# Column quarters of TensorE for the recurrence's diagonal and lower levels, and fp32 attention values by column halves

## What is computed

```python
def _chunked_gated_recurrence(q, k, v, log_f, s0):
    '''S_t = diag(f_t) S_{t-1} + k_t v_t^T ; o_t = S_t^T q_t (per head), chunkwise exact.'''
...
        b = jnp.cumsum(lc, axis=2)
        o = jnp.einsum('bhtd,bhde->bhte', qc * jnp.exp(b), S)
...
        a = jnp.einsum('bhtd,bhsd,bhtsd->bhts', qc, kc, decay)
        o = o + jnp.einsum('bhts,bhse->bhte', a, vc)
...
def _sink_attention(q, k, v, mask, sinks):
    s = jnp.einsum('bnqkgd,bnskd->bnkgqs', q, k) * scale
...
    m = jnp.maximum(jnp.max(s, axis=-1, keepdims=True), sink)
    p = jnp.where(valid, jnp.exp(s - m), 0.0)
    denom = jnp.sum(p, axis=-1, keepdims=True) + jnp.exp(sink - m)
    return jnp.einsum('bnkgqs,bnskd->bnqkgd', p / denom, v)
```

## Time and profile before

| | us |
|---|---|
| median of 3 runs | 1123.98 (1123.93 to 1124.26) |
| profiled execution | 1123.76 |
| its span | 1121.9 |
| PE busy in it | 1085.6 (97%) |
| DVE, POOL, ACT busy | 615.8, 436.7, 399.2 |

### The profile page before, as it was taken

One profiled execution on the slowest core, in us unless ns is written; L12 is line 12 of the kernel. 1 busy time (PEld: TensorE's weight loads), 2 busy tenths in 40 slices (PEclk: granted clock), 3 DMA queues, 4 the chain that ended last, 5 costly groups with the idle time before them and its releaser, 6 DMA issues.

```text
span 1121.9 us, 18648 instructions
## 1 busy us (share of the span) xinstructions
PE 1085.6 (97%) x7464; PEld 1046.8 (93%) x7464; DVE 615.8 (55%) x1222; ACT 399.2 (36%) x807; POOL 436.7 (39%) x294
## 2 busy tenths in 40 slices
PE   6999999999999999999999999999989999999996
PEld 4899999999999999999999999999989999888896
DVE  7143636363635353544673225447677777987835
ACT  4412121212121212354433222431017767755522
POOL 1245454545353535361114452243544433332233
PEclk9999999999999999999999999999999989999999
DMA  7111111111111111101123342321112113232103
GB/s 269 39 38 39 59 39 60 38 60 38 60 39 59 39 60 38 60 20 60 50 88 114 131 135 75 125 69 57 39 39 80 60 58 89 77 80 66 46 26 126
DMA packets 39797, 76.85 MB, mean 69 GB/s; under 512 B 5792, under 2 KB 24736, under 8 KB 39584
## 3 DMA queue, kind: packets, MB, share of 16 engines
q1 hardware_dynamic: 39712, 75.67, 20.7%
HBM read 58.12 MB, written 17.54 MB: 67 GB/s over the span
## 4 chain that ended last, share of the span: by engine, by line
PE 77%; DVE 11%; ACT 7%; issue 2%; POOL 1%; DMA 0%; DVEq 0%; SPq 0%; ACTq 0%; POOLq 0%
PE G L1569 51%; PE R L1619 6%; PE G L1815 4%; ACT SP L982 4%; DVE SP L1407 3%; PE R L1607 2%; DVE PTL L1423 2%; DVE QNL L1392 2%; PE R L1668 1%; PE R L1661 1%; PE R L1635 1%; PE R L1646 1%; PE R L1596 1%; PE R L1628 1%; PE R L1654 1%
## 5 line engine op out<-in xcount | busy, mean ns | idle before, releaser
L1569 PE MATMUL G<-XH,WH 128*128 128x344 f32 x1176 | 385.5, 328 | 1.9 <-DVE RAWF L1078 1.9
L1569 PE MATMUL G<-XL,WH 128*128 128x344 f32 x1176 | 377.9, 321 | 2.3 <-DVE KE L1377 1.9
L1569 PE MATMUL G<-XH,WL 128*128 128x344 f32 x744 | 237.7, 319 | 0.0
L1569 PEld LDWEIGHTS G<-XL,WH 128*128 128x128 f32 x1176 | 221.7, 189 | 5.0 <-DVE WL L1068 2.2
L1569 PEld LDWEIGHTS G<-XH,WH 128*128 128x128 f32 x1176 | 221.9, 189 | 4.3 <-issue 2.1
L612 POOL TENSOR_TENSOR WL<-WR,WH 128x1024 fp32r<-128x1024 f32 x40 | 102.2, 2556 | 181.7 <-ACT WH L757 181.7
L757 ACT ACTIVATE WH<-WR 128x1024 fp32r<-128x1024 f32 x58 | 61.1, 1055 | 289.7 <-PE G L1569 195.2
L1569 PEld LDWEIGHTS G<-XH,WL 128*128 128x128 f32 x744 | 139.8, 188 | 0.0
L1569 PE MATMUL G<-XL,WL 128*128 128x344 f32 x432 | 139.1, 322 | 0.0
L643 POOL TENSOR_TENSOR K<-K,FP 128x512 f32<-128x512 f32 x48 | 78.1, 1628 | 122.2 <-PE R L1619 122.2
L695 POOL TENSOR_TENSOR SP<-SP,small 128x1024 f32<-128x1024 f32 (+1 forms) x32 | 57.3, 1791 | 134.7 <-DVE small L1418 134.7
(11 more groups left out here) (259 smaller groups left out, 2161.0 us busy)
## 6 DMA issues: line engine op xcount, KB each, us to landing
WR<-w SPq DMA_DIRECT2D x58, 512.0 KB, 3.7
A<-x SPq DMA_DIRECT2D x8, 516.0 KB, 8.7
RESO<-x SPq DMA_DIRECT2D x8, 516.0 KB, 5.0
h_spill<-H SPq DMA_DIRECT2D x8, 516.0 KB, 2.9
gate_spill<-EV SPq DMA_DIRECT2D x24, 172.0 KB, 1.9
RES<-h_spill SPq DMA_DIRECT2D x24, 172.0 KB, 2.6
y<-H SPq DMA_DIRECT2D x24, 172.0 KB, 1.9
SS<-states SPq DMA_DIRECT2D x8, 512.0 KB, 3.5
```

Of the source, the lines that this page charges most:

```text
L1569: return nc.tensor.matmul(G[unit_bank(NU * n + i)][:, 0:TU], w[:, n % 3, k, :], x[:, seg(i)], start=(k == 0 and p == 0), stop=(k == KT - 1 ...
```

## The change

The diagonal and levels 1 to 4 (h = 2 to 16) compute, per chunk, only the four blocks of 32 keys against the queries of the same 32 tokens: each a matmul of its own with at most 32 weight columns, whose output lies on the PSUM partitions of that quarter (0, 32, 64, 96). Level 5 (h = 32) goes by two halves of 64 tokens with 32 weight columns each. Level 6 is unchanged. `QM` is laid out by quarters (32 queries, 16 odd ones). DVE's merges read the new layout with as many elements as before. All five R banks are cleared by DVE at the start, since the merges read rows that no matmul has written.

In the attention the values are taken as fp32 from one copy: V in `VP`, the probabilities in `PT`. Each key block has two matmuls, one per half of heads, with 64 weight columns and output on PSUM partitions 0 to 63 or 64 to 127. ACT copies the turned block before (`copy_before`), DVE the own (`copy_own`), each waiting for its transposes and for the values that last read `PT`. The zero fields, the low parts and their subtractions are gone.

```diff
     G3 = sb("G3", [P, T], fp32, [ra[0]])
-    QM = sb("QM", [P, NC, 192], fp32, ra)
+    QM = sb("QM", [P, 4 * NC, 48], fp32, ra)
     r1 = [ra[0]]
...
     rb_[0] += 2 * 4 * SEQ
-    VPH, VPL = sb("VPH", [P, NC, 192], fp32r, rb_), sb("VPL", [P, NC, 192], fp32r, rb_)
+    VP = sb("VP", [P, NC, P], fp32, [rb_[0]])
+    rb_[0] += 2 * 4 * NC * 192
     WXH, WXL = sb("WXH", [P, 2, HK, P], fp32r, [rb_[0]]), sb("WXL", [P, 2, HK, P], fp32r, [rb_[0] + 4 * T])
     EV, EV2 = sb("EV", [P, T], fp32, rb_), sb("EV2", [P, T], fp32, rb_)
     rk = [rb_[0]]
     RES = [sb(f"RES{i}", [P, T], fp32, rb_) for i in range(2)]
     rc = [rb_[0]]
     SP_ = [sb(f"SP{i}", [P, 4, 256], fp32, rb_) for i in range(2)]
-    PTH, PTL = sb("PTH", [P, 2, 512], fp32r, rb_), sb("PTL", [P, 2, 512], fp32r, rb_)
+    PT = sb("PT", [P, 2, 512], fp32, rb_)
     QNH, QNL = sb("QNH", [P, 2, 2, P], fp32r, rb_), sb("QNL", [P, 2, 2, P], fp32r, rb_)
...
         return t[:, 2 * p:2 * p + 2, nb * P:(nb + 1) * P]
+
+    def before_count(q):
+
+        return q - q // NC

...

-        def turned_high(q):
-            for kb in key_blocks(q):
-                act.wait_ge(pt_done, pt_count(q, kb))
-                if q:
-                    act.wait_ge(pv_done, q)
-                nc.scalar.activation(PTH[:, kb, :], R[2 + kb][:], ACT.Copy).then_inc(pth_done, 1)
+        def copy_before(q):
+
+            if q % NC:
+                act.wait_ge(pt_done, pt_count(q, 0))
+                act.wait_ge(pv_done, q)
+                nc.scalar.activation(PT[:, 0, :], R[2][:], ACT.Copy).then_inc(pt_before, 1)

...

-            b = bank(r, f"D{i}")[:, 0:2 * 192].rearrange("p (c w) -> p c w", c=2)
-            at = AT[:, 2 * i:2 * i + 2]
+            b = bank(r, f"D{i}")[:, 0:2 * 192].rearrange("p (c v w) -> p c v w", c=2, v=4)
+            at = AT[:, 2 * i:2 * i + 2].rearrange("p c (v w) -> p c v w", v=4)
             dve.wait_ge(group_done, group_value(r, f"D{i}"))
             if READ_COUNT[f"D{i}", r] > 2:
                 dve.wait_ge(read_dve, READ_COUNT[f"D{i}", r] - 2)
-            nc.vector.copy_predicated(at, imask[:].unsqueeze(1).broadcast_to([P, 2, P]), b[:, :, 0:P]).then_inc(read_dve, 1)
+            nc.vector.copy_predicated(at, imask[:].rearrange("p (v w) -> p v w", v=4).unsqueeze(1).broadcast_to([P, 2, 4, 32]),
+                                      b[:, :, :, 0:32]).then_inc(read_dve, 1)
             dve.wait_ge(read_dve, READ_COUNT[f"D{i}", r] - 1)
-            nc.vector.copy_predicated(at[:, :, 1:P:2], lmask[:, 0, :].unsqueeze(1).broadcast_to([P, 2, P // 2]),
-                                      b[:, :, P:192]).then_inc(read_dve, 1)
+            nc.vector.copy_predicated(at[:, :, :, 1:32:2],
+                                      lmask[:, 0, :].rearrange("p (v w) -> p v w", v=4).unsqueeze(1).broadcast_to([P, 2, 4, 16]),
+                                      b[:, :, :, 32:48]).then_inc(read_dve, 1)

...

+        for b in R:
+            nc.vector.memset(b[:], 0.0)
         nc.vector.memset(ones[:], 1.0)
...
                 if j == 0 and i == 0:
-                    for c in range(2):
-                        dve.wait_ge(vp_high, c + 1)
-                        view = [t[:, 4 * c:4 * c + 4].rearrange("p c (z w) -> p c z w", z=3)[:, :, 0:3:2, :]
-                                for t in (VPH, VPL)]
-                        nc.vector.tensor_tensor(view[1], R[3 + c][:].rearrange("p (c v w) -> p c v w", c=4, v=2),
-                                                view[0].bitcast(fp32), ALU.subtract).then_inc(vp_done, 1)
                     dve.wait_ge(v_turned, 3)
...

-        def turned_rest(q):
-            for kb in key_blocks(q):
-                dve.wait_ge(pth_done, pt_count(q, kb))
-                nc.vector.tensor_tensor(PTL[:, kb, :], R[2 + kb][:], PTH[:, kb, :].bitcast(fp32), ALU.subtract
-                                        ).then_inc(pt_read, 1)
+        def copy_own(q):
+
+            dve.wait_ge(pt_done, pt_count(q, 1))
+            if q:
+                dve.wait_ge(pv_done, q)
+            nc.vector.tensor_copy(PT[:, 1, :], R[3][:]).then_inc(pt_own, 1)

...
                     at = 2 * i + c
-                    ins = nc.tensor.matmul(b[:, c * 192:(c + 1) * 192], K[r % 2][:, at * P:(at + 1) * P], QM[:, at, :],
-                                           start=True, stop=True)
+                    for v in range(4):
+                        ins = nc.tensor.matmul(b[32 * v:32 * v + 32, 192 * c + 48 * v:192 * c + 48 * v + 48],
+                                               K[r % 2][:, at * P + 32 * v:at * P + 32 * v + 32], QM[:, 4 * at + v, :],
+                                               start=True, stop=True)
                 ins.then_inc(group_done, 1)
...
             b = open_group(r, f"L{l}")
+            w = max(32, 2 * h)
             for c in range(NC):
-                cols = slice(c * P, (c + 1) * P)
-                keys = slice(c * P, (c + 1) * P - h)
-                ins = nc.tensor.matmul(b[0:P - h, c * 64:(c + 1) * 64].rearrange("p (n h) -> p n h", h=h),
-                                       K[r % 2][:, keys],
-                                       by_blocks(QU[:, cols], l)[:, :, 1, :], start=True, stop=True)
+                for v in range(P // w):
+                    first = c * P + v * w
+                    ins = nc.tensor.matmul(b[v * w:v * w + w - h, first // 2:(first + w) // 2].rearrange(
+                                               "p (n h) -> p n h", h=h),
+                                           K[r % 2][:, first:first + w - h],
+                                           by_blocks(QU[:, first:first + w], l)[:, :, 1, :], start=True, stop=True)
             ins.then_inc(group_done, 1)
...
             for kb in key_blocks(q):
-                if q:
-                    pe.wait_ge(pt_read, pt_count(q - 1, 1))
+                if kb and q:
+                    pe.wait_ge(pt_own, q)
+                if not kb and q > 1:
+                    pe.wait_ge(pt_before, before_count(q - 1))
                 for i in range(4):
...
             p, nb = query(q)
-            pe.wait_ge(pt_read, pt_count(q, 1))
+            pe.wait_ge(pt_own, q + 1)
+            if nb:
+                pe.wait_ge(pt_before, before_count(q))
             if q:
                 pe.wait_ge(gated, q)
-            steps = [(v, kb, a, b) for kb in key_blocks(q) for v in range(2)
-                     for a, b in ((VPH, PTH), (VPH, PTL), (VPL, PTH))]
-            for n, (v, kb, a, b) in enumerate(steps):
-                ins = nc.tensor.matmul(R[4][:, 0:2 * P].rearrange("p (j w) -> p j w", j=2),
-                                       a[:, nb - 1 + kb, 64 * v:64 * v + P],
-                                       b[:, kb, :].rearrange("p (j v w) -> p j v w", j=2, v=2)[:, :, v, :],
-                                       start=(n == 0), stop=(n == len(steps) - 1))
+            blocks = key_blocks(q)
+            for kb in blocks:
+                for v in range(2):
+                    rows = slice(64 * v, 64 * v + 64)
+                    ins = nc.tensor.matmul(R[4][rows, 0:2 * P].rearrange("p (j w) -> p j w", j=2),
+                                           VP[:, nb - 1 + kb, rows],
+                                           PT[:, kb, :].rearrange("p (j v w) -> p j v w", j=2, v=2)[:, :, v, :],
+                                           start=(kb == blocks[0]), stop=(kb == 1))
             ins.then_inc(pv_done, 1)
```

More of the change, by code:

```diff
@@ L1111, in first_query @@
                 dve.wait_ge(group_done, group_value(r - 1, "O1"))
[L1112 to L1116 removed]
+            odd = QM[:, :, 32:48]
+            gates = FG[:, 0:SEQ].rearrange("p (c n two) -> p c n two", n=16, two=2)
+            nc.vector.tensor_tensor(odd, QM[:, :, 1:32:2], gates[:, :, :, 1], ALU.mult).then_inc(q1_done, 1)
+            qu = QU[:].rearrange("p (c n two) -> p c n two", n=16, two=2)
+            nc.vector.tensor_tensor(qu[:, :, :, 0], QM[:, :, 0:32:2], gates[:, :, :, 0], ALU.mult)
             dve.wait_ge(q1_done, r + 1)
@@ L1322, in _ @@
         nc.vector.tensor_tensor(KE[:], KE[:], KE2[:], ALU.add).then_inc(k_rot, 1)
-        for t in (VPH, VPL):
-            ins = nc.vector.memset(t[:, :, 64:128].bitcast(fp32), 0.0)
-        ins.then_inc(kb_zero, 1)
         prepare(N_KV + 2)
```

25 lines of the change are left out of this document (8 added, 17 removed).

## The result

The changed kernel takes **1075.4 us** (median of 4 runs, 1073.5 to 1076.8) against 1123.95 before: ratio 0.957, 95% interval 0.955 to 0.959, a gain of 48.5 us. The forecast was 1094 with a range from 1085 to 1152. The profiled execution took 1076.7 us with a span of 1074.9.

The account below looks back on a forecast made before the run. PE was taken to bound the kernel, except in the second half of the attention, where a loop through DVE and ACT sets the step. 1123.8 - 23.4 (recurrence) - 6 (attention) = 1094.4 us, range 1085 to 1152.

Parts of the forecast that it names:

- Cost of one pass: PE passes: load 0.8 ns a weight column plus 8, feed 0.84 ns a moving column; 33 ns load taken for every level.
- I expect pairs: Diagonal and levels 1 to 5: two passes run together, 16 ns a pass (diagonal 21.5); -2.93 us a head, -23.4 for eight.
- rivals 2 to 4: Loads don't share, 1126 us (chance 0.18); nothing overlaps, 1150 (0.13); a quarter's load doesn't hide behind a running matmul, 1217 (0.07).
- The switch: Changing the array's shape for the diagonal and levels 1 to 5 costs PE +0.16 us a group.
- Merging, rescaling, clears: POOL and DVE work around the levels and five added PSUM clears cost nothing; uncovered clears at most 3.4 us.
- The values on PE: Attention values: 8 passes as 5 feeds, 1.08 us, plus 0.33 for two switches, 1.41 against 1.43: no change on PE.
- The late step: Second-half attention: DVE's part falls from 1.28 to 0.68 us, PE's own step is 6.28; ten steps save 0.55 each, 5.5 us.
- Sum: Whole kernel: 1123.8 - 23.4 (recurrence) - 6 (attention) = 1094.4 us.
- first rival: The forecast itself, pairs run together: 1085 to 1108 us, its lower end by half-load steps for every width; chance 0.60.

Follow-up runs that it names:

- experiment 10: experiment 6's kernel with level 6 in two matmuls of 32 keys (column quarters 0 and 1) instead of one of 64: 1059.6 us in one run.
- experiment 3: The changed kernel with levels 1 to 5 doing all eight chunks of one quarter before the next quarter: 1108.9 us in one run.
- experiment 5: The changed kernel with level 5 multiplying only 16 of the 32 keys of each half (output incomplete): 1073.0 us in one run.
- experiment 4: The changed kernel with levels 1 to 5 taking two chunks on one quarter before the next quarter: 1077.9 us in one run.
- Experiment 7: The changed kernel with POOL dividing only the last 32 keys of each head (output differs), DVE's order unchanged: 1062.0 us in one run.
- experiment 6: The changed kernel with DVE's minima of step s+2 moved ahead of the query cut and the slice's cut: 1062.6 us, ratio 0.945 to the kernel before.
- experiment 9: The kernel before, with only DVE's minima of step s+2 moved ahead of the query cut and the slice's cut: 1113.0 us, ratio 0.990.
- experiment 2: The kernel before with only the attention values' part of the change (fp32 values by column halves): 1120.1 us, ratio 0.9965.

## Why the prediction failed, step by step

**Cost of one pass: right, but for two details.** The feed (0.84 ns a column) holds within 2 ns: 43/4 = 10.8 ns in the diagonal, 54/2 = 27 against 28 in experiment 10. The load holds for a quarter alone: 30, 28 and 25 ns for 30, 28 and 24 columns (experiment 3) against 31, 29.5 and 26; for 16 columns it is 25 and not 20. The sum, though, took 33 ns for every level, since a quarter may cost its whole width. The starts in the changed kernel's trace tell this apart. They come in fours, one pass of each quarter, and in the second half of a level in twos. Over four starts it takes (ns):

| | weight columns | up to the 33rd pass | behind it | one quarter alone (experiment 3) |
|---|---|---|---|---|
| diagonal | 32 | 43 | 43 | |
| level 1 | 30 | 30 | 33 | 30 |
| level 2 | 28 | 28 | 33 | 28 |
| level 3 | 24 | 25 | 33 | 25 |
| level 4 | 16 | 25 | 33 | 25 |

In the first half of a level a pass thus costs its quarter exactly what it costs there alone: narrower loads do count, and the engine does a pass every 6.3 to 7.5 ns. In the second half four starts take 33 ns, 8.3 a pass, whatever the columns; in between 20 to 40 ns are lost once. Those 33 ns are not the load of a whole width: the same columns load in 25 to 30 in the first half, and 16 columns on two groups go at 29 (experiment 5). So it looks like a pace common to all quarters; that is argued and was not tested, and why it sets in behind the 33rd pass stays open.

**The step that failed: "I expect pairs".** The prediction had the passes of a quarter next to each other, starts in order, hence two at a time and half of the larger of load and feed. The runs showed that as many passes run together as there are column groups: four in the diagonal and levels 1 to 4, two in level 5, in level 6 of experiment 10 and in the values. The terms by group, from the product before to the second product behind, forecast and measured (us a head):

| | forecast | measured |
|---|---|---|
| diagonal | -0.93 | 2.96 to 1.26, -1.69 |
| level 1 | -0.44 | 2.08 to 1.17, -0.91 |
| level 2 | -0.40 | 1.95 to 1.07, -0.88 |
| level 3 | -0.35 | 2.00 to 1.15, -0.85 |
| level 4 | -0.25 | 1.90 to 1.14, -0.76 |
| level 5 | -0.56 | 1.70 to 1.14, -0.56 |

Where only two groups exist the pair model gives the right number, elsewhere it is short by a factor of two on each pass: 63 x (0.016 - 0.0087) = 0.46 is level 1's whole miss. The sum is -5.65 a head (a head's period fell from 56.34 to 50.67), -45.2 instead of -23.4. The rivals 2 to 4, all on the other side, fell: loads of different quarters overlap with each other and with running matmuls. What holds the quarters apart inside is shown only from outside. The starts of the diagonal come in fours 7 ns apart, a four every 43 ns, though the program has the two passes of a quarter next to each other; experiments 3 and 4 show that a pass can start about three places ahead of its turn, not sixteen. Whether each quarter has a short queue of its own, or the engine looks ahead in a common one, stays open.

The row that misled was the scores': on two row halves "pairs" and "as many as there are groups" are the same. A reader of that row could have kept both. The Trainium skill, "TensorEngine Tiling (Array Packing)", Key Properties, says plainly that different tiles load and multiply in parallel, and names no limit of two; the trace now agrees for four column tiles. "TensorE: Matmul & The Clock Gate", Part 3, has starts of different tiles about 4 ns apart, here 7; its sentence that loads overlap running matmuls only where row groups differ (elsewhere in that Part a background weight buffer is excepted) is contradicted by 8.3 ns a pass on one row group.

**The switch: right.** First passes of the levels start 0.25 us behind the product before (0.15 in the kernel before), of the diagonal 0.18 (0.11). The second product comes 0.37 to 0.40 behind the last pass (0.30 to 0.32 before; level 2, with transposes behind it, 0.28 and 0.22). Both together are 0.14 to 0.18 a group, forecast 0.16. **Merging, rescaling, clears: right at nothing.** The five clears hide; PE's first pass came no later.

**The values on PE: a small miss, with the same cause.** Forecast 1.41 against 1.43, no change. Measured from the product before to the transposes: 1.27 us against 1.59, and to the second transpose, whose start comes later now, 1.43 against 1.70. Strict order gave five feeds for the eight passes, since only the second pass of one half could run beside the first of the other; in fact both halves run side by side from the start, which is four. The starts lie in twos, and from the first to the last it is 0.705 us where the prediction named 0.86. One feed of 0.215 less, with the two switches as forecast, is 1.19, or -0.24: that is nearly the whole difference. It shows as -0.27 in each step that PE bounds; eleven of the first 16 steps gained 0.26 to 0.35 each, 3.1 us together.

**The late step: failed.** Forecast 6.83 to 6.28 or 6.23, -5.5 us in ten steps; measured 6.82. DVE did save the 0.6 us, and the next instruction on DVE lost them. The prediction named the query cut only as something queued behind, at a fixed price; its price depends on POOL: the cut reads two operands from SBUF and lasts until 0.28 us behind POOL's division. Experiment 7 shows that it is the division, 6 that it is the place of the cut, 9 that the removed subtractions were not what the steps waited for. The Trainium skill, "Advanced Engine Details and Errata", GPSIMD Details, says that POOL shares a read and a write interface with DVE and conflicts with DVE instructions that have two SBUF inputs; the traces agree (1.41 against 0.42 us), `AR`, with two SBUF inputs as well, was held in the same way, and the copy and the minima, with an input from PSUM, were not. Which property of the cut counts was not varied by itself. By that sentence the row of before (0.81 us for a cut that takes 0.42 alone) could have been read in time; the trace of before even has three cuts of 1.41 us, at 904.65, 960.03 and 1015.10, each ending 0.28 us behind the division, where DVE came to the cut early. And the view with the 6.8 us behind `PTL` has 9.1 us at the scores as well, which the prediction did not read.

**Sum.** -45.2 for the recurrence and the -3.4 of experiment 2 are -48.6, measured are -48.5. That they meet to a tenth is luck: the four runs lie at 1073.5, 1074.1, 1076.7 and 1076.8, with the granted clock, and the median falls between. The profiled execution, one of the slower, gained 47.0 in span. It has 3.4 us at half clock at 705 us that the one of before lacks, and 10.2 us instead of 6.8 around 870 us, each worth about 1.5.

**Slips in the prediction's numbers.** 272 more passes a head should be 256 (5 x 48 and 16), and the trace has 1928 more in all, 256 for each head less 120 in the values. The lower end of the first rival, -28.8 and -8 us, is 1087 and not 1085. Neither moves the forecast.

**The best version** is experiment 6, 1062.6 us, 61.4 under the kernel before; experiment 10, seen in one run only, is at 1059.6. There the change to the values pays in all steps (5.96 against 6.23 in experiment 9), and the recurrence is what it was.

## What to carry to other kernels

Small fp32 matmuls on separate column groups ran together here, as many as there are groups. A pass then cost the larger of one group's load and its feed, divided by the groups in use, but not less than 8.3 ns in the later half of a long row, and as long as neighbours in the program stood on different groups or only a few passes apart. A row of matmuls that switched the array's shape paid 0.14 to 0.18 us for it. And before an instruction is shortened on an engine that is waited for, look whether the next one on it is held by another engine: DVE operations with both inputs in SBUF lasted here until POOL's running operation was over, and moving one of them behind the work that others wait for gave 14 us (some 1.5 of them by the clock), four times what the whole change to the values had given.

## What the runs showed of the hardware that was not expected

- Four column quarters: 6.3 to 7.5 ns a pass with 16 to 30 weight columns up to the 33rd pass of a row, 8.3 behind it, in quarters that take turns. In the mean of level 1 that is 8.7 ns; 10.2 with four passes of a quarter in a row; 25.9 with sixteen.
- One quarter alone has a floor of 25 ns from start to start (24 and 16 weight columns alike); the engine as a whole goes down to 6.3 in the mean of a four.
- A query cut of 0.42 us lasted 1.41 beside a division on POOL, ending 0.28 us behind it; the division kept its 1.89.
- The granted clock fell to its lower level (0.5 of full, 1.2 of 2.4 GHz) at 837, 916 and 1117 us of the kernel before. The changed kernel has these three at the same stages (794, 869 and 1067 us, the second 10.2 us long instead of 6.8) and two more of 3.4 us, at 40 and 705 us. The 4 runs of the changed kernel spread with the clock (1073.5 with a mean of 0.991, 1076.8 with 0.985). Ahead of 705 us PE had stood idle for over half of the first stretch shown (stretch, length, busy, clock):

```profile
701.50:705.00 3.50, 1.58 (x10) 1.33 (x10) 2.14 (x4) 1.06 (x1) 0.14 (x1) 1.00 0.00 0
705.00:706.00 1.00, 1.00 (x7) 1.00 (x6) 0.96 (x4) 0.00 (x0) 0.00 (x0) 0.72 0.57 139
706.00:708.00 2.00, 2.00 (x9) 2.00 (x8) 1.97 (x2) 0.00 (x0) 1.08 (x1) 0.50 0.50 201
709.00:712.50 3.50, 3.50 (x24) 3.50 (x23) 2.15 (x1) 0.29 (x1) 3.17 (x2) 1.00 0.00 0
```

Products were 287 ns apart in it instead of 158; 3.4 us of it cost about 1.5.
